# A two-layer decoder trunk on one core: residual held transposed, RMS factors applied to results, FFN in two passes, 512+256-column split matmuls

## What is computed

```
x += 1/2 * SwiGLU_a(RMSNorm(x))         w_in 1024 x 5632 (gate | up), w_out 2816 x 1024
x += W_out concat(group_1, group_2)     w_in about 1024 x 3584, w_out 1024 x 1024
x += 1/2 * SwiGLU_b(RMSNorm(x))
rms_norm(x) = x * rsqrt(mean(x*x, over channels) + 1e-6) * gain
swiglu = (silu(h @ w_gate) * (h @ w_up)) @ w_out
```

## Time and profile before

| | |
|---|---|
| three runs, us | 1080.5, 1082.59, 1082.97; median 1082.59 |
| profiled execution, span from first to last instruction | 1075.4 us |
| PE, PEld, DVE, ACT busy | 1028.6, 957.5, 577.1, 477.2 us |
| moved by DMA | 183.79 MB, mean 171 GB/s |
| mean granted TensorE clock | 0.991 |

### The profile page before, as it was taken

One profiled execution on the slowest core, in us unless ns is written; L12 is line 12 of the kernel. 1 busy time (PEld: TensorE's weight loads), 2 busy tenths in 40 slices (PEclk: granted clock), 3 DMA queues, 4 the chain that ended last, 5 costly groups with the idle time before them and its releaser, 6 DMA issues.

```text
span 1075.4 us, 17437 instructions
## 1 busy us (share of the span) xinstructions
PE 1028.6 (96%) x7220; PEld 957.5 (89%) x7223; DVE 577.1 (54%) x605; ACT 477.2 (44%) x575; POOL 29.9 (3%) x43
## 2 busy tenths in 40 slices
PE   5999999899998999999899999998999889999997
PEld 4999999799997999999799999996998779999996
DVE  4445454685485445454645454547556654454544
ACT  4434344574364444344534444344535544343442
POOL 2000000000000000000000000003001000000000
PEclk9999999999999999999999999999999989999999
DMA  9474554564335464654554655645552443746551
GB/s 321 161 233 151 200 189 162 173 200 157 118 119 194 140 233 154 197 190 161 172 186 144 221 169 182 200 152 177 157 158 79 136 144 132 230 143 211 178 173 39
DMA packets 137145, 183.79 MB, mean 171 GB/s; under 512 B 3028, under 2 KB 122008, under 8 KB 136984
## 3 DMA queue, kind: packets, MB, share of 16 engines
q1 hardware_dynamic: 135792, 179.51, 50.6%
q10 hardware_dynamic: 1224, 3.75, 1.0%
q0 software_dynamic: 96, 0.03, 0.0%
HBM read 182.24 MB, written 1.05 MB: 170 GB/s over the span
## 4 chain that ended last, share of the span: by engine, by line
PE 90%; DVE 5%; ACT 2%; POOL 1%; issue 1%; DMA 1%; DVEq 0%; POOLq 0%; SPq 0%; ACTq 0%
PE ch L915 20%; PE ch L917 20%; PE ch L916 20%; PE acc L915 9%; PE acc L916 9%; PE acc L917 9%; DVE w_lo L588 1%; DVE x_lo L617 1%; ACT w_hi L376 1%; DVE xn L609 1%; DMA xs<-in_x 1%; POOL act L345 1%; PE ch L957 1%; ACT xn L393 1%; PE acc L1046 1%
## 5 line engine op out<-in xcount | busy, mean ns | idle before, releaser
L915 PE MATMUL ch<-x_hi,w_hi 128*128 128x256 f32 x1760 | 502.1, 285 | 4.8 <-DVE x_lo L617 3.3
L916 PE MATMUL ch<-x_lo,w_hi 128*128 128x256 f32 x1760 | 499.3, 284 | 0.0
L917 PE MATMUL ch<-x_hi,w_lo 128*128 128x256 f32 x1760 | 499.3, 284 | 0.0
L588 DVE TENSOR_TENSOR w_lo<-raw,w_hi 128x2048 fp32r<-128x2048 f32 x163 | 374.6, 2322 | 141.0 <-ACT w_hi L376 140.7
L376 ACT ACTIVATE w_hi<-raw 128x2048 fp32r<-128x2048 f32 x168 | 320.3, 1908 | 131.7 <-PE acc L917 131.7
L915 PEld LDWEIGHTS ch<-x_hi,w_hi 128*128 128x128 f32 x1760 | 339.3, 193 | 10.0 <-DVE x_lo L617 3.6
L916 PEld LDWEIGHTS ch<-x_lo,w_hi 128*128 128x128 f32 x1760 | 339.2, 193 | 2.0 <-issue 0.2
L917 PEld LDWEIGHTS ch<-x_hi,w_lo 128*128 128x128 f32 x1760 | 339.0, 193 | 0.0
L643 DVE TENSOR_TENSOR act<-ch,mix 128x256 f32<-128x256 f32 x88 | 37.4, 425 | 268.9 <-PE ch L917 268.9
L915 PE MATMUL acc<-w_hi,y_hi 128*128 128x512 f32 x416 | 163.4, 393 | 0.4
L916 PE MATMUL acc<-w_lo,y_hi 128*128 128x512 f32 x416 | 162.7, 391 | 0.0
(11 more groups left out here) (167 smaller groups left out, 491.4 us busy)
## 6 DMA issues: line engine op xcount, KB each, us to landing
raw<-in_ffn_w_in SPq DMA_DIRECT2D x88, 1024.0 KB, 5.4
raw<-in_ffn_w_out SPq DMA_DIRECT2D x44, 1024.0 KB, 4.9
raw<-in_ab_w_in SPq DMA_DIRECT2D x14, 1024.0 KB, 5.0
raw<-in_cd_w_in SPq DMA_DIRECT2D x14, 1024.0 KB, 5.4
raw<-in_ab_w_out SPq DMA_DIRECT2D x4, 1024.0 KB, 4.8
raw<-in_cd_w_out SPq DMA_DIRECT2D x4, 1024.0 KB, 5.0
gains<-in_ffn_norm ACTq DMA_DIRECT2D x4, 512.0 KB, 3.7
cst<-in_consts SPq DMA_DIRECT2D x1, 1216.0 KB, 13.2
```

The source lines that it names most:

```text
L588: v.tensor_tensor(w_lo[:, pos, :], raw[:, pos, :], w_hi[:, pos, :].bitcast(F32), ALU.subtract).then_inc(lo_done, 1)
L915: pe.matmul(dst, l_hi, r_hi, start=start, stop=False, skip_group_check=True)
L916: pe.matmul(dst, l_hi, r_lo, start=False, stop=False, skip_group_check=True)
L917: return pe.matmul(dst, l_lo, r_hi, start=False, stop=stop, skip_group_check=True)
```

## The change

The residual is held as `xT`, channels on partitions and tokens along the free axis, from the beginning (16 transposes at the start, 16 at the end). A phase's output is made in this layout too: in all output projections the weights are the stationary operand. The RMSNorm gain, now a number per partition, is applied as the next input is split, tile of 128 channels by tile, as soon as that tile of `xT` is complete. The RMS factor, a number per token, is no longer in the input: squares are summed over the tiles (`squares` on ACT, `add_square` on DVE), one small matmul with ones sums over partitions (`mean_square`), POOL raises to the power -1/2, DVE puts the factors on a diagonal, and a matmul with ones spreads them as a row over all partitions (`token_rows`). The row `rb` multiplies every result of an input projection as DVE moves it out of PSUM (`evacuate`); in an FFN it multiplies the gate and the output.

An FFN has two passes: first all gate and up (22 slots), with the hidden layer kept whole in SBUF as `y_ffn` (hi and lo side by side), then all of w_out (four groups of 256 output channels, each in three slots of 8, 8 and 6 row tiles). Its products use `two`: one matmul of 512 columns, `w_hi` by (hi, lo) together, and one of 256, `w_lo` by hi. The two halves of the result are added later, ACT copying one half (`second_halves`) and DVE adding. Mixers keep three matmuls of 256 columns (`three`), now also in the output projection; those of their inputs that need tokens on partitions use 512-column weights. In the mixers the evacuations move from ACT to DVE, the order of slots and small products is rewritten, and the silu, sigmoid and tanh follow the evacuation on ACT. The FFN loops become straight code. `ch` is used in two pairs of banks by turns (`ch_free`), `acc` for the small products alone.

```diff
+YK = F // P
+PARTS = [(0, 8), (8, 16), (16, 22)]
...
-        xs = sb("xs", [P, T, D])
-        xn = sb("xn", [P, T, D])
+        xT = sb("xT", [P, KD, S])
+        x_hl = sb("x_hl", [P, KD, 2, S], F32R)
+        y_mix = sb("y_mix", [P, KD, 2, S], F32R)
         act = sb("act", [P, KD, S])
-        x_hi = sb("x_hi", [P, KD, S], F32R)
-        x_lo = sb("x_lo", [P, KD, S], F32R)
-        y_hi = sb("y_hi", [P, KD, S], F32R)
-        y_lo = sb("y_lo", [P, KD, S], F32R)
-        mix = sb("mix", [P, 15, H * S])
+        tb = sb("tb", [P, 2, 2, S])
+        tt = sb("tt", [P, 2, S])
...
+            def second_halves(p, g):
+                ae.wait_ge(chunk, 2 * g + 2)
+                ae.activation(tb[:, g % 2, :, :], ch[:, banks(g):banks(g) + 2, S:2 * S], ACT.Copy).then_inc(b_out, 2)
...
+            def next_input(m, d):
+
+                ae.wait_ge(x_new, 8 * (m - 1) + d + 1)
+                if m < 6:
+                    ae.activation(x_hl[:, d, 0, :], xT[:, d, :], ACT.Copy, scale=norm_gain(m, d)).then_inc(xh_ready, 1)
+                squares(m, d)
...
+            def ffn(p):
+                n, g, fi = SLOT0[p], GROUP0[p], ITER * ffn_index(p)
+                for i in range(ITER):
+                    second_halves(p, g + 2 * i)
+                    round_slot(n + 2 * i + 3)
+                    ae.wait_ge(g_ready, fi + i + 1)
+                    ae.activation(sg[:, :, :], tt[:, :, :], ACT.Silu).then_inc(s_ready, 1)
+                    second_halves(p, g + 2 * i + 1)
+                    round_slot(n + 2 * i + 4)
+                    ae.wait_ge(h_ready, fi + i + 1)
+                    ae.activation(y_ffn[:, 2 * i:2 * i + 2, 0, :], ut[:, :, :], ACT.Copy).then_inc(yh_ready, 1)
+                for q in range(4):
+                    last = n + 2 * ITER + 3 * q + 2
+                    round_slot(last + 1)
+                    round_slot(last + 2)
+                    if p == 0 and q == 0:
+                        lower_bound()
+                    second_half(p, g + 2 * ITER + q, 0)
+                    second_half(p, g + 2 * ITER + q, 1)
+                    if q < 3:
+                        round_slot(last + 3)
+                    next_input(p + 1, 2 * q)
+                    next_input(p + 1, 2 * q + 1)
+                    if q == 3:
+                        round_slot(last + 3)
+
...
+                y_split([(4, 6, 1), (6, 8, 2)])
                 for s in (12, 13):
-                    chunks(0, s, (lambda j: b_bg[:, 2 * s - 24 + j, :], ACT.Copy, 1.0))
-                    y_split([(2 * s - 20, 2 * s - 18, s - 10)])
-                for s in (14, 15, 16):
-                    after(0, s)
+                    evacuated(ab_group(s))
+                    h = slice(2 * (s - 12), 2 * (s - 12) + 2)
+                    ae.activation(b_g[:, h, :], b_g[:, h, :], ACT.Silu).then_inc(gs_ready, 1)
+                    y_split([(2 * s - 24, 2 * s - 22, s - 9)])
+                    if s == 12:
+                        round_slot(n + 16)
...
+            def mean_square(m):
+                v.wait_ge(rs_mm, m + 1)
+                v.tensor_scalar(msum, (acc if m < 6 else ch)[:, 3, 0:T], EPS, None, ALU.add).then_inc(ms_ready, 1)
+
+            def token_diag(m):
+                v.wait_ge(rc_ready, m + 1)
+                for t in range(T):
+                    ins = v.tensor_scalar(diag[:, t * P:(t + 1) * P], ident, rcol[:, t:t + 1], None, ALU.mult)
+                ins.then_inc(dg_ready, 1)
+
+            def token_rows(m):
+                v.wait_ge(rb_mm, m + 1)
+                own(v.tensor_copy(rb[:, :], acc[:, 2, 0:S]))
+                v.sem_inc(rb_ready, 1)
+
...
+            def ffn(p):
+                n, g, fi = SLOT0[p], GROUP0[p], ITER * ffn_index(p)
+                for i in range(ITER):
+                    a = banks(g + 2 * i)
+                    sum_pair(p, g + 2 * i)
+                    own(v.tensor_tensor(tt[:, :, :], ch[:, a:a + 2, 0:S], tb[:, (g + 2 * i) % 2, :, :], ALU.add))
+                    v.sem_inc(ch_free[(g + 2 * i) % 2], 2)
+                    if i == 0:
+                        token_rows(p)
+                    v.tensor_tensor(tt[:, :, :], tt[:, :, :], both(rb[:, :]), ALU.mult).then_inc(g_ready, 1)
+                    rest(n + 2 * i + 3)
+                    a = banks(g + 2 * i + 1)
+                    sum_pair(p, g + 2 * i + 1)
+                    own(v.scalar_tensor_tensor(out=ut[:, :, :], in0=ch[:, a:a + 2, 0:S], scalar=1.0, in1=tb[:, (g + 2 * i + 1) % 2, :, :], op0=ALU.mult, op1=ALU.add))
+                    v.sem_inc(ch_free[(g + 2 * i + 1) % 2], 2)
+                    v.wait_ge(s_ready, fi + i + 1)
+                    v.scalar_tensor_tensor(out=ut[:, :, :], in0=ut[:, :, :], scalar=0.5, in1=sg[:, :, :], op0=ALU.mult, op1=ALU.mult).then_inc(h_ready, 1)
+                    rest(n + 2 * i + 4)
+                    v.wait_ge(yh_ready, fi + i + 1)
+                    v.tensor_tensor(y_ffn[:, 2 * i:2 * i + 2, 1, :], ut[:, :, :], y_ffn[:, 2 * i:2 * i + 2, 0, :].bitcast(F32), ALU.subtract).then_inc(y_ready, 1)
+                for q in range(4):
+                    last = n + 2 * ITER + 3 * q + 2
+                    rest(last + 1)
+                    rest(last + 2)
+                    if p == 0 and q == 0:
+                        lower_bound()
+                    gq = g + 2 * ITER + q
+                    for j in range(2):
+                        d = 2 * q + j
+                        v.wait_ge(b_out, b_count(p, gq, j))
+                        own(v.tensor_tensor(tt[:, j, :], ch[:, banks(gq) + j, 0:S], tb[:, gq % 2, j, :], ALU.add))
+                        v.sem_inc(ch_free[gq % 2], 1)
+                        own(v.tensor_tensor(tt[:, j, :], tt[:, j, :], rb[:, :], ALU.mult))
+                        own(v.tensor_tensor(xT[:, d, :], xT[:, d, :], tt[:, j, :], ALU.add))
+                        v.sem_inc(x_new, 1)
+                    if q < 3:
+                        rest(last + 3)
+                    new_input(p + 1, q)
+                    if q == 3:
+                        end_of_phase(p, last + 3)
+
+            def new_input(m, q):
+                for d in (2 * q, 2 * q + 1):
+                    if m < 6:
+                        low_input(m, d, xT[:, d, :])
+                    add_square(m, d)
+
+            def end_of_phase(p, n):
+                mean_square(p + 1)
+                if p + 1 < 6:
+                    token_diag(p + 1)
+                    rest(n)
+
...
+                rest(n + 5)
+                cumulate(0)
+                cumulate(1)
+                rest(n + 6)
+                keys(0)
+                keys(1)
+                evacuate(ab_group(4), b_q[:, 0:2, :])
...
+                y_rest([(4, 6, 1), (6, 8, 2)])
+                for pp in range(2):
+                    h = slice(2 * pp, 2 * pp + 2)
+                    v.wait_ge(hg_rs, 2 * pp + 2)
+                    own(v.tensor_tensor(b_o[:, h, :], b_o[:, h, :], b_rs[:, h, :], ALU.mult))
+                for pp in range(2):
+                    h = slice(2 * pp, 2 * pp + 2)
+                    if pp:
+                        evacuate(ab_group(13), b_g[:, 2:4, :])
+                        rest(n + 16)
+                    v.wait_ge(gs_ready, pp + 1)
+                    v.tensor_tensor(act[:, h, :], b_o[:, h, :], b_g[:, h, :], ALU.mult).then_inc(y_f, 1)
+                    y_rest([(2 * pp, 2 * pp + 2, 3 + pp)])
...
-            def three(dst, l_hi, l_lo, r_hi, r_lo, start, stop):
-                pe.matmul(dst, l_hi, r_hi, start=start, stop=False, skip_group_check=True)
-                pe.matmul(dst, l_hi, r_lo, start=False, stop=False, skip_group_check=True)
-                return pe.matmul(dst, l_lo, r_hi, start=False, stop=stop, skip_group_check=True)
-
-            def channels(dst, pos, j):
-                c = slice(j * P, (j + 1) * P)
+            def w_at(w, n, k, j):
+                return w[:, n % RING, k * PAIR + j * P:k * PAIR + (j + 1) * P]
+
+            def two(bank, n, k, j, rhs, start, stop):
+
+                pe.matmul(ch[:, bank, :], w_at(w_hi, n, k, j), rhs.rearrange("p a s -> p (a s)"), start=start, stop=False, skip_group_check=True)
+                return pe.matmul(ch[:, bank, 0:S], w_at(w_lo, n, k, j), rhs[:, 0, :], start=False, stop=stop, skip_group_check=True)
+
+            def three(bank, n, k, j, rhs, start, stop):
+                dst = ch[:, bank, 0:S]
+                pe.matmul(dst, w_at(w_hi, n, k, j), rhs[:, 0, :], start=start, stop=False, skip_group_check=True)
+                pe.matmul(dst, w_at(w_hi, n, k, j), rhs[:, 1, :], start=False, stop=False, skip_group_check=True)
+                return pe.matmul(dst, w_at(w_lo, n, k, j), rhs[:, 0, :], start=False, stop=stop, skip_group_check=True)
+
...
+            def mean_square(m):
+                pe.wait_ge(ssq_done, m + 1)
+                for t in range(T):
```

(55 more changed lines are left out.)

1286 lines of the change are left out of this document (667 added, 619 removed).

## The result

The changed kernel takes 1049.94 us (median of 4 runs, 1048.97 to 1050.92) against 1082.2 for the kernel before beside it: a ratio of 0.9715, 95% interval 0.9689 to 0.9741. The forecast was 1034. So the kernel is faster by 32 us, where 48 were expected.

What follows compares the result with a forecast made beforehand. TensorE, busy 1028.6 of 1075.4 us, was taken as the bound. Start, phases, clock and end summed to a span of 1027.4 us, -48; with the distance of 7.2 kept, the time was 1034 us, range 1020 to 1050.

Steps and rivals of the forecast that it cites:

- Price of a matmul: FFN products: a 512+256 pair costs 0.347 us against 0.360 for three of 256, saving 13.3 ns each, 28 us in all.
- FFN: FFN 1, 2 and 3 take 184.0, 184.3 and 184.0 us, against 195.0, 196.9 and 196.7 before.
- the cover of 4 to 6 us: FFN input pass: freed bank pairs and rests are ready 4 to 6 us before they are needed.
- Between the phases: After an FFN's last matmul 0.3 us of wait stays of 6.7 or more; after a mixer nothing stays.
- Start: TensorE ends slot 2 near 32.0, and FFN 0 ends at 199 us (196 to 204) against 207.5.
- ab: Mixer phase ab takes 129.6 us against 127.5, with 7.5 us of new waits; edges 122 and 137.
- cd: Mixer phase cd takes 136.7 us against 145.0, with 4.5 of tail stalls and 0.5 for rotary; edges 131 and 142.
- Clock: Half clock behind two new stalls of about 3 us costs 1.6 us in all (0 to 3).
- Rival A: Mixers' in-order queues are worse: every stall doubles, with cold clock after each, +12 us, 1046; chance 0.12.
- Tail: The kernel's end, from residual steps and transposes to output, takes 8.2 us against 6.8.
- Base: The profiled span lies 7.2 us below the median time, a distance kept: 1082.6 - 48 = 1034.6 us.
- Rival D: FFN input pass becomes bound by handovers between ACT and DVE: step 13.6 not 11.1 us, +110, 1144; chance 0.03.

Runs made afterwards that it cites:

- the run made for this: Changed kernel plus small float32 products of constants (one or two of 1 column, one of 256) in input slots of FFN 1 to 3: 1074.64 us.
- the combined order with the early sum: Changed kernel with new orders of tails, start and ab's evacuations, cosines on DVE, sum over partitions still in slot 0: 1032.33 us.

## Why the prediction was right or wrong

- **Price of a matmul.** Right as a saving (20 of the 28 us), with two corrections: in the output pass the third product would have cost 6.7 ns more and not 13.3, and an input pass has two paces. FFN 0's was the slower: 352 x 6.7 = 2.35 us of its miss of 8.3. That is chance as far as these runs show, since the same order also ran at the faster pace.
- **FFN.** FFN 1 was right to 0.1 us, the added products (0.4 and 0.45 forecast, 0.45 and 0.43 measured) too, and the cover of 4 to 6 us: no wait in any pass behind its head but at slot 2 of FFN 0. In FFN 3 I left out that 12 of the 16 transposes of the output lie in its last pass, 12 x 0.12 = 1.4 us.
- **Between the phases.** The mechanism was right: the gaps of 6.7 us are gone, and to couple the phases again costs 41 us. The size failed: at the head of ab DVE began 0.3 us late behind `w_lo`, two steps of three cost 0.58 and not 0.43, and the rest and the square of tile 6 stood ahead of tile 7's, so the sum of squares was ready for TensorE at 5.5 us and not at 4.5. TensorE waited 1.2, 1.7 and 1.2 us behind the three FFNs, not 0.3. FFN 2's 1.4 us are this.
- **Start.** The step that failed most. Forecast: slot 2 done at 32.0. I priced w_lo of slot 2 but not what stands behind it on DVE: group 0's sum came after the sum of squares, mean square and diagonal, so slot 2 waited 3.4 us for its banks, and half clock followed. A better order gives 4.3 us back. The first product came at 15.0 and not 12.5, since the last of the small loads let PE begin at 10.85; with x's transposes first it comes at 13.1 to 13.5.
- **ab.** The stalls were right within 0.5 us (8.0 for 7.5). The sum at the head (1.2) and 1.7 us of half clock were missing.
- **cd.** The tail's 4.5 were 5.1, and the sum at the head cost 1.2. Rotary's wait, for which I had 0.5, was 1.2, because DVE stood still for 2 us behind GpSimd twice. Most of the miss of 6.4 is the clock: 10.2 us at half clock in cd, where TensorE was busy all but a little, which I estimate at 5.1 us of loss. Together this is 7.6, so the other terms of cd were some 1 us too dear. DVE's standstill stood in the trace of before, where one w_lo has 6705 ns beside the median of 2286, during GpSimd's copy of 6.60 us; I read the mean of the group and not its maximum.
- **Clock.** I had 1.6 us in all. The trace after has 17 us of it in busy stretches behind stalls, some 8 us of loss. The stalls of 3.4 to 3.9 us were each followed by a stretch of it. The longest, 6.8 us in cd, begins within the four products of 4 rows behind rotary, after a wait of only 1.1; with that wait down to 0.2 us 3.4 us of half clock are left there (758.6 to 762.0), so this one is not the price of a stall alone, and what sets it stays open. The clock is a large part of what ab and cd missed. Rival A named it, with 12 us, and its 1046 was nearest to the result, by luck in part: its stalls of double length did not come (8.0 for 7.5 and 5.1 for 4.5).
- **Tail.** 10.5 for 8.2: steps of 0.58 again, and half clock.
- **Base.** The distance of 7.2 us was no distance but a fast execution: its own is about 2. This error went the other way, so the time's miss of 16 us looks better than the span's of 21.6.
- **Rival D.** Its handovers never bound an input pass: behind slot 2 of FFN 0, TensorE waits in no FFN's input pass but at its head.

The terms: FFN 0 8.3, ab 3.3, FFN 2 1.4, cd 6.4, FFN 3 1.5, tail 2.3, less the clock's 1.6, make 21.6. So the steps that failed are DVE's queue at the start, which was left unpriced, and the clock's 1.6 us, which should have been some 8.

## What to carry to other kernels

When work leaves TensorE for DVE and ACT, lay out every in-order queue around each handover, the short steps too: here another order, with two products moved from GpSimd to DVE and no work removed, gave 25 us more, some 2 of them FFN 0's pace. Stalls of 3.5 us cost half as much again in the clock behind them, so price both; and in every group of the profile read the longest instruction beside the mean.

## What the runs showed that I had not expected

- A stream of 512 and 256 column products with their loads has two stable paces, 346.7 and 353.3 ns a pair at granted clock 1.00 and no wait. In FFN 1 a float32 product of one column between changed it every time; two of them, or one of 256 columns, left the faster pace or brought it in the run made for this, but one of 256 columns brought the slower in others.
- A third product of 256 columns costs 13.3 ns more than the shared one in the input pass, 6.7 in the output pass, on the same shapes.
- A DVE subtraction of 2.29 us takes 4.37 beside a GpSimd product of 2.40.
- TensorE's idle time of 5.4 to 7.3 us at each of five places, with half clock behind it, cost 41 us in all.
- Executions of one kernel can lie 7 us apart (1029.5 to 1036.3 us for the combined order with the early sum), and FFN 0's pace differed between executions of the same order.
